# Two transformer blocks on one core: operand tiles rewritten behind the last product that reads them, first sums on other engines, two weight blocks left unsplit

## The reference

```
mod = silu(c) @ w_ada + b_ada                     # shift, scale, gate
h   = rms_norm(x, g_pre) * (1 + scale) + shift
proj = h @ w_in                                   # 20032 columns
a   = latent_attention(...) * silu(z_mla);   y_mla = a @ w_mla_proj
b   = dilated_attention(...) * silu(z_dil);  y_dil = b @ w_dil_proj
merged = sigmoid(gl_mla) * y_mla + sigmoid(gl_dil) * y_dil
x = x + gate * rms_norm(merged @ w_o, g_post)     # block one

y = indexed_attention(x, top 64 keys) * silu(g) @ w_out_a
x = layer_norm(4**.25 * x + y);  x += (p[0] @ w_ple) * sigmoid(x @ w_ple_gate)
q, g, k, v = x @ w_q_b, x @ w_kv_b                # block two, second layer
y = stick_breaking(q, k, v) * silu(g) @ w_out_b
x = layer_norm(4**.25 * x + y);  x += (p[1] @ w_ple) * sigmoid(x @ w_ple_gate)
```

## Time and profile before

| what | value |
|---|---|
| median of 3 runs | 2494.61 us (2494.29 to 2499.43) |
| the profiled execution | 2497.27 us, its span 2496.0 us |
| TensorE busy | 2379.6 us, 95% of the span |
| VectorE busy | 1498.6 us, 60% |
| ScalarE busy | 1137.7 us, 46% |
| GpSimd busy | 101.6 us, 4% |
| TensorE on the chain that ended last | 80% of the span |
| weights and other data moved | 470.55 MB, mean 189 GB/s |
| mean granted TensorE clock | 0.984 |

### The profile page before, as it was taken

One profiled execution on the slowest core, in us unless ns is written; L12 is line 12 of the kernel. 1 busy time (PEld: TensorE's weight loads), 2 busy tenths in 40 slices (PEclk: granted clock), 3 DMA queues, 4 the chain that ended last, 5 costly groups with the idle time before them and its releaser, 6 DMA issues.

```text
span 2496.0 us, 28114 instructions
## 1 busy us (share of the span) xinstructions
PE 2379.6 (95%) x11212; PEld 1983.6 (79%) x11212; DVE 1498.6 (60%) x2087; ACT 1137.7 (46%) x1484; POOL 101.6 (4%) x117
## 2 busy tenths in 40 slices
PE   6899999999999999999997999999899999999988
PEld 4567888878888887878887878878788888887877
DVE  6887565444545445776755675565655455455564
ACT  4333444434444454443343444554445545455443
POOL 0000000000000000000000100000100001011010
PEclk9999999999999999999998999999899999999989
DMA  9886543435553457887564545545456555554644
GB/s 344 317 314 242 166 143 124 156 127 188 191 184 113 144 174 250 301 270 253 170 196 141 171 153 168 161 153 186 160 185 186 169 175 164 184 168 152 195 151 152
DMA packets 133541, 470.55 MB, mean 189 GB/s; under 512 B 15537, under 2 KB 15793, under 8 KB 132385
## 3 DMA queue, kind: packets, MB, share of 16 engines
q1 hardware_dynamic: 130688, 458.42, 55.8%
q0 software_dynamic: 1424, 9.37, 1.0%
q10 hardware_dynamic: 1298, 0.97, 0.2%
HBM read 466.60 MB, written 2.10 MB: 188 GB/s over the span
## 4 chain that ended last, share of the span: by engine, by line
PE 80%; DVE 6%; ACT 4%; issue 1%; DMA 1%; POOL 0%; ACTq 0%; DVEq 0%
PE G L464 24%; PE G L466 24%; PE G L465 24%; PE A L537 4%; DVE wlo L378 2%; PE A L809 1%; PE A L785 1%; ACT whi L376 1%; ACT dil L492 1%; PE A L985 1%; DVE CP L1733 0%; DMA raw<-in_weights 0%; DVE dil L1727 0%; PE A L1444 0%; PE A L951 0%
## 5 line engine op out<-in xcount | busy, mean ns | idle before, releaser
L378 DVE TENSOR_TENSOR wlo<-raw,whi 128x1024 fp32r<-128x1024 f32 (+2 forms) x784 | 938.7, 1201 | 757.2 <-ACT whi L376 754.8
L376 ACT ACTIVATE whi<-raw 128x1024 fp32r<-128x1024 f32 (+2 forms) x784 | 802.6, 1026 | 879.0 <-PE G L466 765.2
L464 PE MATMUL G<-whi,XH 128*128 128x512 f32 (+3 forms) x2808 | 1095.7, 390 | 40.7 <-DVE wlo L378 17.9
L466 PE MATMUL G<-whi,XL 128*128 128x512 f32 (+3 forms) x2808 | 1074.6, 383 | 0.0
L465 PE MATMUL G<-wlo,XH 128*128 128x512 f32 (+3 forms) x2808 | 1074.5, 383 | 0.0
L464 PEld LDWEIGHTS G<-whi,XH 128*128 128x128 f32 x2808 | 531.8, 189 | 142.3 <-DVE wlo L378 20.7
L466 PEld LDWEIGHTS G<-whi,XL 128*128 128x128 f32 x2808 | 531.3, 189 | 96.5
L465 PEld LDWEIGHTS G<-wlo,XH 128*128 128x128 f32 x2808 | 532.3, 190 | 90.9 <-issue 0.5
L464 PE MATMUL A<-whi,XH 128*128 128x512 f32 x168 | 71.8, 427 | 19.4 <-DVE wlo L378 13.8
L328 DVE CUSTOM_DVE_ANT_0 raw<-raw,dil 128x1024 f32<-128x1024 f32 x64 | 80.8, 1277 | 0.0
L465 PE MATMUL A<-wlo,XH 128*128 128x512 f32 x168 | 66.5, 396 | 0.0
(11 more groups left out here) (195 smaller groups left out, 1620.6 us busy)
## 6 DMA issues: line engine op xcount, KB each, us to landing
raw<-in_weights SPq DMA_DIRECT2D x792, 512.0 KB, 4.2
raw<-in_weights SPq DMA_DIRECT2D x80, 384.0 KB, 3.1
raw<-in_weights SPq DMA_DIRECT2D x16, 288.0 KB, 2.8
raw<-in_weights SPq DMA_DIRECT2D x8, 336.0 KB, 2.9
FT<-in_xT SPq DMA_DIRECT2D x4, 512.0 KB, 5.7
Xn<-in_x POOLq DMA_DIRECT2D x1, 2048.0 KB, 11.6
GG<-in_ln_g POOLq DMA_DIRECT2D x2, 1024.0 KB, 7.6
CP<-in_ln_b POOLq DMA_DIRECT2D x2, 1024.0 KB, 5.1
```

What stands on the lines that cost most here:

```text
L376: th = AC.mark(nc.scalar.activation(h[:, 0:2 * cols], r[:, 0:2 * cols], ACT.Copy))
L378: tl = VE.mark(nc.vector.tensor_tensor(l[:, 0:2 * cols], r[:, 0:2 * cols], h[:, 0:2 * cols].bitcast(F32), ALU.subtract))
L464: nc.tensor.matmul(o, h, wh, start=(k == start), stop=False)
L466: ins = nc.tensor.matmul(o, l, wh, start=False, stop=(k == nkt - 1))
```

## The change

Five edits are in the difference.

1. Slots 0 and 1, the first two of the program, are in `WHOLE`. They read `FT` as soon as it is written (`whole_ready`), and `operand_rows` writes the `FT` tiles of a group first and the `XH` copies after them.
2. The squares of x stand between the four SiLU copies on ScalarE, and the three additions of the quarters move from VectorE to GpSimd.
3. A step of `rows_to_x` waits for `x_read[k]`, the last slot that read its own two tiles, in place of the end of the whole product. Steps are therefore written between the slots of that last product, by `behind`: four in the last gate product, two in the last q product of each attention, four in the last product of `ple`. The side work is emptied before that product in `ple`.
4. After `ple` the remaining steps are fewer (two, not four) before the last rows of the new x are turned.
5. `topk_task` gives the queue back after two, four and six rounds.

```
-WHOLE = frozenset([*range(12, 22, 2), *range(24, 66, 4)])
+WHOLE = frozenset([0, 1, *range(12, 22, 2), *range(24, 66, 4)])
...
-                PE.wait(ready[k])
+                PE.wait(whole_ready[k] if s in WHOLE else ready[k])
...
+            if xh is XH:
+                x_read[k0] = t
...
             t_sq = act_copy(sqx[:, s4, :], FT[:, s4, :], [d_x[n]], ACT.Square)
             if n:
-                VE.wait(t_sq, t)
-                t = VE.mark(nc.vector.tensor_tensor(sqx[:, 0:4, :], sqx[:, 0:4, :], sqx[:, s4, :], ALU.add))
+                GP.wait(t_sq, t_sum)
+                t_sum = GP.mark(nc.gpsimd.tensor_tensor(sqx[:, 0:4, :], sqx[:, 0:4, :], sqx[:, s4, :], ALU.add))
...
-                th = act_copy(h, h, [tm[k - lo]], ACT.Identity, bias=mods[:, k:k + 1])
-                t2 = act_copy(XH[:, k, :], h, [th])
+                whole_ready[k] = act_copy(h, h, [tm[k - lo]], ACT.Identity, bias=mods[:, k:k + 1])
+            for k in range(lo, hi):
+                h = FT[:, k, :]
+                t2 = act_copy(XH[:, k, :], h, [whole_ready[k]])
...
+        def behind(steps, count):
+            yield
+            for _ in range(count):
+                next(steps)
+                yield
...
             for k in range(lo, hi, 2):
-                AC.wait(x_used, *ft_tok[k], *ft_tok[k + 1])
+                AC.wait(x_read[k], *ft_tok[k], *ft_tok[k + 1])
...
-                VE.wait(th, x_used)
+                VE.wait(th, x_read[k])
...
-        ready = [None] * KT
         drain_all()
-        steps = rows_to_x(ready)
-        next(steps)
-        next(steps)
+        nready = [None] * KT
+        steps = rows_to_x(nready)
+        gate_chunk(1, 3, behind(steps, 4))
...
-                    if rnd == 4:
+                    if rnd in (2, 4, 6):
                         yield [t]
...
-            pair, t = gemm(512, KT, XH, XL, ready)
+            if c == 3:
+                rows = [None] * KT
+                steps = rows_to_x(rows)
+            pair, t = gemm(512, KT, XH, XL, ready, steps=behind(steps, 2) if c == 3 else None)
...
+                    trail = behind(steps, 4)
+                pair, t = gemm(512, KT, XH, XL, ready, look=2 if c == 0 else 0, steps=trail)
```

More of the change, by code:

```diff
@@ L438, in next_pair @@
             return pair
+        x_read = [None] * KT
         def gemm_slot(pair, cols, k0, nkt, xh, xl, ready, start=0, look=0):
@@ L585, in first_and_second_block @@
         t_cs = []
+        t_sum = None
         for n in range(4):
-            t = PE.mark(nc.tensor.matmul(A[n].t[:, :], ones[0:1, :], crow[:, 512 * n:512 * n + 512],
-                                         start=True, stop=True))
-            t_cs.append(act_copy(cs[:, 512 * n:512 * n + 512], A[n].t[:, :], [t], ACT.Silu))
+            c_read = PE.mark(nc.tensor.matmul(A[n].t[:, :], ones[0:1, :], crow[:, 512 * n:512 * n + 512],
+                                              start=True, stop=True))
+            t_cs.append(act_copy(cs[:, 512 * n:512 * n + 512], A[n].t[:, :], [c_read], ACT.Silu))
             A[n].free = [t_cs[-1]]
-        c_read = t
-        ada["c"] = [[t_cs[1], d_cols], [t_cs[3], d_cols]]
-        t = None
-        for n in range(4):
             s4 = slice(4 * n, 4 * n + 4)
@@ L598, in first_and_second_block @@
             if n:
-                VE.wait(t_sq, t)
-                t = VE.mark(nc.vector.tensor_tensor(sqx[:, 0:4, :], sqx[:, 0:4, :], sqx[:, s4, :], ALU.add))
-            else:
-                t = t_sq
+                GP.wait(t_sq, t_sum)
+                t_sum = GP.mark(nc.gpsimd.tensor_tensor(sqx[:, 0:4, :], sqx[:, 0:4, :], sqx[:, s4, :], ALU.add))
+            else:
+                t_sum = t_sq
+        ada["c"] = [[t_cs[1], d_cols], [t_cs[3], d_cols]]
+        t = t_sum
         PE.wait(t)
@@ L616, in first_and_second_block @@
         ready = [None] * KT
+        whole_ready = [None] * KT
         first = [G[0:2], G[2:4]]
@@ L1194, in first_and_second_block, with gate_chunk @@
         gl_free = [list(rel)]
-        def gate_chunk(g, c):
-            pair, t = gemm(512, KT, XH, XL, ready)
+        def gate_chunk(g, c, steps=None):
+            pair, t = gemm(512, KT, XH, XL, ready, steps=steps)
             gl_t[g][c] = []
@@ L1254, in rows_to_x @@
                 yield
-        ready = [None] * KT
+        for g, c in ((0, 2), (0, 3), (1, 0), (1, 1), (1, 2)):
+            gate_chunk(g, c)
         drain_all()
-        steps = rows_to_x(ready)
-        next(steps)
-        next(steps)
+        nready = [None] * KT
+        steps = rows_to_x(nready)
+        gate_chunk(1, 3, behind(steps, 4))
+        ready = nready
         for c in range(4):
@@ L1521, in first_and_second_block, with rest_of_rows, layer_norm @@
         x_used = t
-        def new_rows():
-            r = [None] * KT
-            steps = rows_to_x(r)
-            next(steps)
-            next(steps)
-            def rest_of():
-                drain_all()
-                yield from steps
-            quick_last.append((steps, rest_of()))
-            return r
-        quick_last = []
-        def layer_norm(layer, ready):
+        def rest_of_rows(steps):
+            drain_all()
+            yield from steps
+        def layer_norm(layer, ready, steps):
             nonlocal x_used, ln_loaded
@@ L1544, in layer_norm @@
                 if c == 0:
-                    steps, last_steps = quick_last.pop()
+                    last_steps = rest_of_rows(steps)
                     pairs = [next_pair(), next_pair()]
@@ L1639, in ple @@
                 toks = to_nat(b, pair, t, 512, "pl")
-                pair, t = gemm(512, KT, XH, XL, ready, look=2 if c == 0 else 0)
-                free["ga"] = [*grel[0], *grel[1], free.get("ga_used")]
+                trail = None
                 if not last and c == 3:
                     drain_all()
-                    x_used = t
                     r = [None] * KT
                     steps = rows_to_x(r)
-                    next(steps)
-                    next(steps)
+                    trail = behind(steps, 4)
+                pair, t = gemm(512, KT, XH, XL, ready, look=2 if c == 0 else 0, steps=trail)
+                free["ga"] = [*grel[0], *grel[1], free.get("ga_used")]
                 sg = to_nat(Ga, pair, t, 512, "ga", ACT.Sigmoid)
@@ L1672, in rest_of @@
             def rest_of():
-                for _ in range(4):
+                for _ in range(2):
                     yield next(steps)
@@ L1688, in x_rows @@
                 ft_tok[k] = done
-        ready = layer_norm(0, new_rows())
+        ready = layer_norm(0, rows, steps)
         ready, steps = ple(0, ready, False)
@@ L1771, in first_and_second_block @@
         x_used = t
-        ready = layer_norm(1, new_rows())
+        ready = layer_norm(1, rows, steps)
         outs = ple(1, ready, True)
```

3 lines of the change are left out of this document (removed).

## The result

| what | before | after |
|---|---|---|
| median of 5 runs each | 2497.04 us | 2472.94 us (2469.81 to 2475.72) |
| ratio after to before, 95% interval | | 0.9904 [0.9890, 0.9919] |
| profiled execution, its span | 2497.27, 2496.0 us | 2475.72, 2474.4 us |
| TensorE busy | 2379.6 us | 2372.7 us |
| GpSimd busy | 101.6 us | 110.6 us |

The kernel is 24.1 us faster by the medians, between 20.2 and 27.5 us by the interval. The profiled executions differ by 21.6 us.

What follows compares the result with a forecast made beforehand. TensorE, busy for 95% of the span, was taken to bound the kernel. Boundaries 12.1, selection 3.1 and opening 2.5 summed to 17.7 us, giving 2477 us on the median of 2494.6, range 2470 to 2488.

Steps and rivals of the forecast that it cites:

- w_out_a: Start of w_out_a: wait and half speed gone, 4.4 us, less 1.4 us lateness from VectorE's rotation, steps and splits: 3.0 us.
- the opening: Start of the kernel: GpSimd additions and unsplit slots gain 2.5 us; bounds 1.8 us lost to 3.7 us gained.
- w_mla_proj and w_out_b: Starts of these two products: the 2.5 us wait and 1.7 us of half speed fall away, 4.2 us each.
- The moved steps at nothing: 12 steps inside the last products cost nothing, covered by 1.8 us of slack; uncovered, 1.3 us each.
- the selection's second half: Selection, second half: of a 1.77 us wait, moving two rounds behind the split gains 1.7 us.
- w_q_b: Start of w_q_b: the 1.54 us wait goes, a new 0.85 us wait for additions comes; 0.7 us gain.
- The selection's first half: Selection, first half: two of four rounds move behind the split TensorE awaits for 2.95 us; 1.44 us gain.
- The unsplit slots: Slots 0 and 1 in the opening: first matmul 4.2 us earlier, third slot 2.8 us earlier, with line 609's move.
- the far price: Rival: GpSimd additions take 4.4 us and the opening turns from 2.5 to -1.8; 2481 us, chance 0.15.
- no wait of 2 us came up behind a boundary: Answers the rival that half the waits and half speed remain at three large boundaries: 2483 us, chance 0.13.
- the slots of the last gate product kept their distance: Answers the rival that steps hold up last products, each making its slot 1.3 us late: 2499 us, chance 0.05.
- the steps did start behind single slots: Answers the rival that single-slot tokens bring no earlier start; only selection and opening gain: 2489 us, chance 0.05.

Runs made afterwards that it cites:

- e2_topk: The kernel before with the selection's edit alone (queue given back after two, four and six rounds): 2492.21 us, ratio 0.9976.
- e3_open: The kernel before with the opening edits alone (squares between copies, additions on GpSimd, slots 0 and 1 unsplit): 2493.30 us, ratio 0.9986.
- e6_four: The kernel after with four steps behind the last product before each w_out and the next two steps later: 2475.12 us, ratio 0.9911.
- e1_bounds: The kernel before with the boundary edits alone (steps behind the last reader, side work emptied earlier): 2483.79 us, ratio 0.9950.
- e5_split01: The kernel after with slots 0 and 1 split again: 2473.92 us, ratio to before 0.9910.
- e4_sums_vec: The kernel after with the three additions back on VectorE: 2472.06 us, ratio to before 0.9903.
- e7_all: The kernel after with additions on VectorE, four steps behind last q products, gated part's side work emptied behind its last product and one product earlier: 2469.63 us.

## Why the prediction was right, and where its terms were not

The forecast was 2477 us with 2470 to 2488, measured were 2472.94. The edited stretches of the two profiles differ by 17.7 us, the forecast's sum. The waits fell as the prediction says; that the sums agree to a tenth is luck, since half speed of 1.7 us comes and goes in two of the terms (w_out_a and the opening). Point by point:

- **w_mla_proj and w_out_b**, 4.2 us each: 4.21 and 4.82. The wait and the half speed went together, as the rows above show. All three kernels with the old waits (before, e2_topk, e3_open) have a clock of 0.83 behind them at both places. At w_out_b a wait of 0.48 us inside the product went as well, which I hadn't counted.
- **The moved steps at nothing**: right at the places where they were put (slots 2.72 us apart). e6_four shows the limit: two more of them cost 0.6 us at w_out_b.
- **w_out_a**, 3.0 us, and the selection's second half, 1.7: 4.50 together, 4.7 expected. The lateness that I put at 1.4 us is 1.50, from the chain that the prediction names. VectorE's rows and GpSimd's, then the slot that waits:

```profile
1656.53 2.18 DVE L378 TENSOR_TENSOR wlo<-raw,whi 128x1024 fp32r<-128x1024 f32 x1
1658.63 0.41 DVE L528 TENSOR_TENSOR rd<-nat,sinT 128x256 f32<-128x256 f32 x1
...
1661.70 0.68 DVE L1260 TENSOR_TENSOR XL<-FT,XH 128x512 fp32r<-128x512 f32 x1
1662.30 1.22 DVE L378 TENSOR_TENSOR wlo<-raw,whi 128x1024 fp32r<-128x1024 f32 x1
```

```profile
1654.62 3.00 POOL L526 TENSOR_TENSOR rc<-nat,cosT 128x512 f32<-128x512 f32 x2 [49.79 <-ACT nat L496]
```

```profile
1663.57 0.50 PE L466 MATMUL G<-whi,XH 128*128 128x512 f32 x1 [1.50 <-DVE wlo L378]
```

  The first split takes 2.18 us beside GpSimd's rotation, 1657.62 being the rotation's end: the turn of some 1 us that the prediction allowed for. But e1_bounds and e2_topk show that the 1.7 us of half speed in the term belong to no single wait. The step "a boundary's price is its wait and its half speed" held at w_mla_proj and w_out_b; at w_out_a it held in this pair of profiles by luck, and there it fails as a rule.
- **w_q_b**, 0.7 us: 0.37 by stretch (0.3 to 1.1 in the six kernels with this edit). The wait that replaces the old one was put at 0.85 us and is 0.84:

```profile
1847.46 1.06 PE L541 MATMUL A<-ident,Xn 128*128 128x128 f32 x8 [0.84 <-DVE Xn L1658]
```

- **The selection's first half**, 1.44 us: 1.43, the wait falls from 2.95 to 1.52 us.
- **The opening**, 2.5 us: 2.41. Line 612 at 20.78 (20.7 forecast), the first matmul at 29.00 (28.7), the third slot at 38.02 (38.5). The addition that no row showed takes 2.44 us alone, for which I took 2.5 from rows 12. The Trainium skill's figure (GPSIMD Engine Reference, "Elementwise — side-by-side cycle accounting"), by which the estimate was 2.25 us, comes out 8% low. The Trainium skill's rule of the lock (SBUF — State Buffer, "SBUF: two separate sides") agrees with 3.29 against 1.28 us.

  That 2.41 meets 2.5 is luck in two ways. In e3_open, e5_split01 and e6_four the same three additions take 8.12 us, not 9.12, and line 612 comes 0.7 to 0.8 us sooner counted from the first matmul, so the turns fall differently from one execution to the next. And with the clock alike the opening gains 4.4 us (e3_open), more than the 3.7 of the prediction's best case.

  The reasoning weighed the additions on GpSimd only against the kernel before. There the squares stood behind all four SiLU copies and VectorE's additions began late:

```profile
12.53 3.89 DVE L600 TENSOR_TENSOR dil<-dil 128x1024 f32<-128x1024 f32 x3 [12.53 <-ACT dil L492]
```

  With squares and copies alternating VectorE begins them at 8.60 us, and TensorE's sum starts 3.9 us sooner than with GpSimd (e4_sums_vec). The gain is the new order's, and the move to GpSimd gives part of it back.

  The unsplit slots, for which the forecast had 2.3 us at the third slot (2.8 less the 0.5 of line 609), bring 0.8 to 1.9 there and nothing that the end shows. The two of them take 9.0 us (9.8 forecast), and between 8.2 (e4_sums_vec) and 9.5 us (e7_all) in other kernels, so the loss to half speed, put at 3.0 us from one profile, isn't a fixed size.

The base accounts for part of the 4 us between forecast and result: the forecast rested on a median of 2494.6, and the kernel before took 2497.0 beside the kernel after. From there it would read 2479.3, and 6.4 us more were gained than its terms hold. In the profiles the unedited stretches give 3.9 of the 21.6 us, and they swing by 6 us between kernels that are the same there. Whether the rest of the 24.1 us is chance or a lasting effect of the shifted stages stays open; the interval reaches down to 20.2.

The rivals: the additions weren't at the far price, no wait of 2 us came up behind a boundary, the slots of the last gate product kept their distance, and the steps did start behind single slots.

## What to carry to other kernels

Let a rewrite of an operand wait for the last reader of its own tile and write it into the queues there, and look in the rows behind the boundary for the next instruction that is late. Before work is moved to an idle engine, ask whether the new order alone would do, and whether the two engines can work side by side. When a lower clock follows waits, count it in the sum over a stage, not in the price of one wait.

## What the runs showed of the hardware

- The half-speed stretches wander. In kernels with the same instructions there, a wait of 2.95 us in the selection was followed by 3.4 us of half speed (e1_bounds) or not (before, e3_open), and one of 2.67 us at w_out_a was (before, e3_open) or wasn't (e2_topk). A wait of some 2 us near 987 us was followed by it in three of eight profiles. Over the twelve profiles the mean clock lies between 0.982 and 0.988, that is 90 to 59 us at half speed (twice the missing share of the span). How much of this is wandering isn't shown, since the kernels differ in their waits.
- The granted clock misses some of it. In the window from 20 to 40 us the kernel after shows 0.69 and 0.80, the kernel before 1.00, though its first matmuls stood as far apart as half speed makes them (the two slots of 8.4 us). Seven of the twelve profiles show 1.00 in this window.
- A VectorE instruction and a GpSimd one that share their turns aren't slowed evenly. In the kernel after one modulation got its turn at once (1.29 us), the next waited (3.29 us). In e3_open and e6_four the first one waited already (3.06 and 2.97 us), and the three additions took 8.12 us there instead of 9.12.
